# Eight-sublayer decoder trunk: the order in which the third and fourth tile of rows take the last four pieces of weights

## Chip, cores and metric

One core of one Trainium2 chip. The time is device microseconds of one execution of the whole program, all weights read from HBM; lower is better.

## What is computed

A trunk of two layers over 512 rows of 1024 float32 values. Each layer is a half-step SwiGLU feed-forward network (FFN, inner width 2816), a token mixer (linear recurrence and differential attention in the first layer, forgetting attention and a convolution in the second), a cross-attention into 256 memory rows, and a second half-step FFN. So eight sublayers end in all, and each is wrapped the same way:

```
h = h + w * RMSNorm_post(f(RMSNorm_pre(h)))
```

Every matrix product is made to nearly float32 precision out of three passes: both operands are split into a rounded part and a rest (`whi`, `wlo` for weights, `xhi`, `xlo` for inputs), and hi·lo, lo·hi and hi·hi are summed.

## The kernel before

**Data.** `h` stays in SBUF as four tiles of 128 rows (`h[:, t, :]`, t = 0 to 3). A piece of weights is two blocks of 128 x 512. SP loads pieces into 4 raw slots (`load`, L522), ScalarE writes `whi` and VectorE `wlo` into 4 split slots (`split`, `split_next`, L783, L1310 where a norm's gain is multiplied in, L779, L1305 where not), three pieces ahead of use. TensorE counts `pieces_used`; ScalarE's split of piece n waits in L776 until piece n - 4 has been used, and VectorE's half follows ScalarE's. SP reloads a raw slot once the low parts of its piece are made.

**A sublayer's last stage.** The product that ends a sublayer (`mix_out`, `xo`, `down`) has two groups, one for each half of the 1024 output columns. A group has four pieces (`down` five), and tile t sums into bank t of the group's four banks. Its second group is written by `last_group` (L2229), which orders TensorE's work by hand for the last four pieces: tile 0 takes all four, then tile 1 takes all four, then come tiles 2 and 3. When a tile is complete `tile_done` is signalled; for tile 3 the last `pieces_used` serves.

**What runs beside it.** `close_sublayer` exists on ScalarE (L840) and VectorE (L1439); both lists are executed strictly in the order written. For each tile: VectorE adds the product to `y_rows` (only for `down`, L1446), ScalarE squares it with a sum (L829), VectorE makes the variance (L1450) and multiplies the post gain in (L1457), GpSimd raises to -1/2 (L680), VectorE updates `h[t]` (L1492). Then TensorE transposes the tile of h (L2140, eight transposes), ScalarE copies the result to `xhi` (`open_hi`, L814) and VectorE makes `xlo` (`open_lo`, L1338): the next sublayer's input. ScalarE also squares the new h (`next_h`, L818) for the next norm. Between these steps stand the splits of the next stage's first pieces. The last group before nothing (`opens` false) has only the updates and stores.

There are two forms of this. Where the next stage is a gate and up stage (`rows` true; three of the seven), the transposes take rows already scaled by their own norm: VectorE adds to the squares (L1526), GpSimd takes the power (L685), ScalarE writes `y_rows` (`scale_rows`, L867), and only then can TensorE transpose (`scaled_units`, L2148). ScalarE's order there is

```
square_tile 0, next_h(0), scale_rows(0), square_tile 1,
split_next,  next_h(1), open_hi(0), scale_rows(1),
split_next,  open_hi(1), square_tile 2,
split_next,  square_tile 3, next_h(2), scale_rows(2), next_h(3), ...
```

Elsewhere (`rows` false, four of the seven) TensorE transposes h itself (`updated_units`, L2143) and ScalarE's order is

```
square_tile 0, next_h(0), square_tile 1, open_hi(0),
split_next,  next_h(1), open_hi(1),
split_next,  square_tile 2, split_next, square_tile 3, ...
```

VectorE's list has the same shape, with `split_next` at the same places; `update(2)` stands behind `add_second(3)`, the addition of tile 3, in both and in the last one. The `split_next` behind square_tile 1 is the one that needs the slot of the first of the last four pieces; the next ones need the second and third.

**The next stage** begins with `first_group` (L2263): each piece takes tiles 0 and 1 first (256 columns, once `xlo` of both is there) and later tiles 2 and 3. The transposes of tiles 2 and 3 stand between its pieces, behind its second and third piece with `rows`, behind its first and second without.

Of the kernel before, what the change touches and what calls it, by code (L numbers as in the profile page):

```python
# [127 lines left out]
def build(nc, A, out):  # L128
# [9 lines left out]
    def place(name, shape, dt=f32, at=None, size=FLOAT):  # L138

        n = (int(np.prod(shape[1:])) * size + 31) // 32 * 32  # L140
        if at is None:
            at = top[0]
            top[0] += n
        assert at + n <= nc.sbuf_usable_end, (name, at + n - nc.sbuf_usable_end)
        return nc.alloc_sbuf_tensor_at(name, shape, dt, offset=at)
# [48 lines left out]
    rows = place("rows", [P, 3, P], f32, at(9984))  # L194
# [64 lines left out]
    def sem(name):  # L259
# [8 lines left out]
    hi_made, lo_made, pieces_used = map(sem, ("hi_made", "lo_made", "pieces_used"))  # L268
# [22 lines left out]
    tile_done, y_ready, y_squared, proj_ready, v_ready, y_mixed = map(sem, (  # L291
        "tile_done", "y_ready", "y_squared", "proj_ready", "v_ready", "y_mixed"))
# [41 lines left out]
    def group_pieces(kind, g, n, arg=None):  # L334

        return 1 if kind == "odd_in" and ODD_COLS[g][0] == "c_f" else \
            n + 2 if arg == "late_kv" and g == 0 else n
# [156 lines left out]
    def x_bank(t, group):  # L494

        return 4 * ((group + t // 2) % 2)
# [1555 lines left out]
    def _(pe):  # L2052
        E = Engine(pe, None)
# [78 lines left out]
        def wait_banks(group):  # L2132
            wait_evicted(group)
            wait_read(group)

        def x_units(t, bank, bs=(0, 1), src=h):

            for b in bs:
                for k in range(4):
                    last = T(x_unit(bank, t, b)[:, k, :], src[:, t, (4 * b + k) * P:(4 * b + k + 1) * P], ident[:])  # L2140
                E.run(last, x_transposed)

        def updated_units(t):  # L2143

            E.await_(h_ready)
            x_units(t, x_bank(t, E.group))

        def scaled_units(t):  # L2148

            E.await_(h_ready)  # L2150
            E.await_(rows_scaled)
            x_units(t, x_bank(t, E.group), src=y_rows)
# [76 lines left out]
        def last_group(bank, n_kp, src_hi, src_lo, ready, opens, rows):  # L2229

            base, lead = E.piece, n_kp - SPLIT_SLOTS

            def piece(kp, tiles):
                weights(base + kp)
                ready(kp)
                return token_major((base + kp) % SPLIT_SLOTS, kp, n_kp, bank, src_hi, src_lo, tiles)
            for kp in range(lead):
                piece(kp, range(TT)).then_inc(pieces_used, 1)
            for t in range(2):
                for kp in range(lead, n_kp):  # L2240
                    last = piece(kp, (t,))
                E.run(last, tile_done)
            E.group += 1
            if opens and not rows:
                wait_banks(E.group)
                updated_units(0)
            for kp in range(lead, lead + 2):
                piece(kp, (2, 3)).then_inc(pieces_used, 1)
                if rows and kp == lead:
                    wait_banks(E.group)  # L2250
                    scaled_units(0)
            if opens and not rows:
                updated_units(1)
            for kp in range(lead + 2, n_kp):
                last = piece(kp, (2,))
                if rows and kp == lead + 2:
                    scaled_units(1)
            E.run(last, tile_done)
            for kp in range(lead + 2, n_kp):
                piece(kp, (3,)).then_inc(pieces_used, 1)  # L2260
            E.piece += n_kp

        def first_group(ended, rows=False):  # L2263
# [89 lines left out]
        def weights(n):  # L2353

            pe.wait_ge(lo_made, n + 1 + RAW_SLOTS)
# [11 lines left out]
        def token_major(slot, kp, n_kp, bank, src_hi, src_lo, tiles):  # L2367

            for i in range(PK):
                k = 2 * kp + i  # L2370
                for t in tiles:
                    toks = slice(t * P, (t + 1) * P)
                    last = three(PS[:, bank + t, :], src_hi[:, k, toks], src_lo[:, k, toks],
                                 whi[:, slot, i, :], wlo[:, slot, i, :], kp + i == 0,
                                 kp == n_kp - 1 and i == PK - 1)
            return last

        def forget_gates(slot, bank):

            w = [t[:, slot].rearrange("p a (b n) -> p (a b) n", n=P) for t in (whi, wlo)]  # L2380
            for k in range(KT):
                last = three(PS[:, bank, :], w[0][:, k, :], w[1][:, k, :], xhi[:, k, :], xlo[:, k, :],
                             k == 0, k == KT - 1)
            return last
# [29 lines left out]
        for n_stage, (kind, l, arg, ng, np_) in enumerate(STAGES):  # L2414
# [41 lines left out]
            for g in range(straight(kind, ng)):  # L2456
# [6 lines left out]
                n_kp = group_pieces(kind, g, np_, arg)  # L2463
# [3 lines left out]
                if ends_sublayer(kind, arg) and g == 1:  # L2467
                    if arg == "late_kv":
                        E.await_(kv_copied)
                    if kind == "down":  # L2470
                        last_group(bank, n_kp, plain_hi, plain_lo,
                                   lambda kp: pe.wait_ge(mid_lo_ready, 2 * (m0 + kp + 1)), opens(n_stage), opens_scaled(n_stage))
                    else:
                        last_group(bank, n_kp, xhi, xlo, lambda kp: pe.wait_ge(xlo_ready, x_ready + 2 * kp + 2),
                                   opens(n_stage), opens_scaled(n_stage))
                    ended = True
                    continue
# [3 lines left out]
                for n_piece in range(n_kp):  # L2481
                    kp = (0, 1, 0, 1, 2, 3)[n_piece] if late else n_piece
# [8 lines left out]
                    if kind == "down":  # L2491
                        pe.wait_ge(mid_lo_ready, 2 * (m0 + kp + 1))
                        last = token_major(slot, kp, n_kp, bank, plain_hi, plain_lo, range(TT))
                    else:
                        pe.wait_ge(xlo_ready, x_ready + (KT if name == "c_f" else 2 * kp + 2))
                        last = forget_gates(slot, bank) if name == "c_f" else \
# [49 lines left out]
            if kind == "even_in":  # L2546
# [17 lines left out]
                for n in range(len(LEVELS) + 1):  # L2564
# [7 lines left out]
                    for half in range(2):  # L2572
                        if n >= 1:
                            pe.wait_ge(level_merged, 2 * n - 1 + half)
                        for b in range(8 * half, 8 * half + 8):
# [3 lines left out]
                            last = mm(blocks_of(level_bank, level_bank + 4)[:, b, :], lhs, rhs, start=True, stop=True)  # L2579
# [172 lines left out]
```

## Time and profile before

| | us |
|---|---|
| median of 3 runs | 2327.05 |
| lowest, highest | 2322.51, 2327.62 |
| the profiled execution | 2327.22 |
| its span, first to last instruction | 2325.4 |
| TensorE busy | 2301.9 |
| VectorE busy | 1313.6 |
| ScalarE busy | 976.0 |
| GpSimd busy | 77.3 |
| mean granted TensorE clock | 0.997 |

PE is TensorE, PEld its weight load, DVE VectorE, ACT ScalarE, POOL GpSimd. A row of a timeline gives the start in the span, the duration, the engine, the line of the kernel and the operation, and in brackets how long the engine sat idle before it and what ended that. Matmuls are pipelined: the next begins before the one before it ends.

### The profile page before, as it was taken

The numbers are of one execution on the slowest core, as the hardware profiler recorded it, in microseconds if no ns is written. First come the engines' busy times: TensorE is split into PE (matmuls) and PEld (weight loads), VectorE is DVE, ScalarE is ACT, GpSimd is POOL, SyncE is SP. The second block draws the span as 40 slices with busy tenths as digits, with TensorE's granted clock in tenths as the row PEclk, the third lists the DMA queues.
The fourth block names the chain that finished last, engine by engine and source line by source line (L and its number), as shares of the span: only waits on it lengthen the run. The fifth ranks groups of instructions, "written<-read, shape, count | busy, mean of one in ns | idle before, by whom it ended". The sixth has DMA issues, their size and how long they took to land. (4 is left out here: it accounts for less than half of the span.)

```text
span 2325.4 us, 30178 instructions
## 1 busy us (share of the span) xinstructions
PE 2301.9 (99%) x11939; PEld 1951.6 (84%) x11939; DVE 1313.6 (56%) x1833; ACT 976.0 (42%) x1618; POOL 77.3 (3%) x115
## 2 busy tenths in 40 slices
PE   8999999999999999999999999999999999999998
PEld 7888888888888888888888888888888888888887
DVE  5756545595645446573355573355895545567434
ACT  4433324444544454443343443344365445344332
POOL 0000004000000000000010000000000000000000
PEclk9999999999999999999999999999999999999999
DMA  4332232311223122423223313233322222331321
GB/s 167 104 132 81 92 109 79 104 63 55 83 76 106 58 83 96 146 72 94 98 91 109 132 50 118 91 96 96 100 74 73 91 64 91 109 127 55 114 95 72
DMA packets 171650, 217.70 MB, mean 94 GB/s; under 512 B 13080, under 2 KB 123000, under 8 KB 171512
## 3 DMA queue, kind: packets, MB, share of 16 engines
q1 hardware_dynamic: 171400, 215.75, 28.8%
q8 instruction: 96, 1.57, 0.3%
q14 instruction: 42, 0.34, 0.0%
q10 hardware_dynamic: 112, 0.03, 0.0%
HBM read 213.63 MB, written 2.10 MB: 93 GB/s over the span
## 5 line engine op out<-in xcount | busy, mean ns | idle before, releaser
L2058 PE MATMUL ps<-xlo,whi 128*128 128x512 f32 (+1 forms) x2056 | 756.7, 368 | 1.7 <-DVE wlo L1310 1.7
L2059 PE MATMUL ps<-xhi,wlo 128*128 128x512 f32 (+1 forms) x2056 | 753.6, 367 | 0.0
L2060 PE MATMUL ps<-xhi,whi 128*128 128x512 f32 (+1 forms) x2056 | 753.5, 366 | 0.0
L1310 DVE SCALAR_TENSOR_TENSOR wlo<-raw,vec,whi 128x512 fp32r<-128x512 f32 (+1 forms) x488 | 340.8, 742 | 397.0 <-ACT whi L783 395.9
L783 ACT ACTIVATE whi<-raw,vec 128x512 fp32r<-128x512 f32 (+1 forms) x488 | 320.8, 709 | 456.7 <-PE ps L2060 394.4
L2058 PEld LDWEIGHTS ps<-xlo,whi 128*128 128x128 f32 x2056 | 389.1, 189 | 64.7 <-issue 2.1
L2059 PEld LDWEIGHTS ps<-xhi,wlo 128*128 128x128 f32 x2056 | 389.1, 189 | 62.4
L2060 PEld LDWEIGHTS ps<-xhi,whi 128*128 128x128 f32 x2056 | 388.9, 189 | 62.6
L1305 DVE TENSOR_TENSOR wlo<-raw,whi 128x1024 fp32r<-128x1024 f32 x104 | 126.8, 1223 | 188.5 <-ACT whi L779 187.7
L779 ACT ACTIVATE whi<-raw 128x1024 fp32r<-128x1024 f32 x104 | 109.5, 1056 | 209.8 <-PE ps L2060 209.3
L2058 PE MATMUL ps<-wlo,xhi 128*128 128x512 f32 x352 | 139.7, 397 | 2.5 <-issue 2.5
L2059 PE MATMUL ps<-whi,xlo 128*128 128x512 f32 x352 | 137.9, 392 | 0.0
L2060 PE MATMUL ps<-whi,xhi 128*128 128x512 f32 x352 | 137.8, 392 | 0.0
L2176 PE MATMUL ps<-wlo,mid_hi 128*128 128x512 f32 x336 | 131.6, 392 | 0.4 <-DVE wlo L1299 0.4
L2180 PE MATMUL ps<-whi,mid_lo 128*128 128x512 f32 x336 | 130.8, 389 | 0.0
L2181 PE MATMUL ps<-whi,mid_hi 128*128 128x512 f32 x336 | 130.8, 389 | 0.0
L2058 PE MATMUL ps<-wlo,plain_hi 128*128 128x512 f32 x320 | 125.0, 391 | 0.0
L2060 PE MATMUL ps<-whi,plain_hi 128*128 128x512 f32 x320 | 124.6, 389 | 0.0
L2059 PE MATMUL ps<-whi,plain_lo 128*128 128x512 f32 x320 | 124.5, 389 | 0.0
L802 ACT ACTIVATE whi<-w 128x512 fp32r<-128x512 f32 x144 | 83.3, 622 | 91.9 <-PE ps L2060 33.9
L1299 DVE TENSOR_TENSOR wlo<-w,whi 128x512 fp32r<-128x512 f32 x144 | 92.9, 685 | 35.3 <-ACT whi L802 34.4
L1736 DVE TENSOR_TENSOR mid<-mid,ps 128x1024 f32<-128x1024 f32 x33 | 40.3, 1221 | 111.9 <-ACT mid L1058 111.9
(279 smaller groups left out, 2842.3 us busy)
## 6 DMA issues: line engine op xcount, KB each, us to landing
raw<-ffn_w_gate_dram SPq DMA_DIRECT2D x176, 256.0 KB, 2.8
raw<-ffn_w_up_dram SPq DMA_DIRECT2D x176, 256.0 KB, 3.1
raw<-ffn_w_down_dram SPq DMA_DIRECT2D x96, 256.0 KB, 3.0
w<-ffn_w_down_dram SPq DMA_DIRECT2D x72, 256.0 KB, 5.2
raw<-xattn_w_kv_dram SPq DMA_DIRECT2D x64, 256.0 KB, 2.9
raw<-even_w_in_dram SPq DMA_DIRECT2D x56, 256.0 KB, 2.9
raw<-odd_w_in_dram SPq DMA_DIRECT2D x42, 256.0 KB, 2.9
raw<-xattn_w_q_dram SPq DMA_DIRECT2D x32, 256.0 KB, 3.0
```

Of the source, the lines that this page charges most:

```text
L779: a(flat(whi[:, slot]), flat(raw[:, from_slot]), ACT.Copy).then_inc(hi_made, 1)
L783: last = a(hi[:, k, :], full[:, k, :], ACT.Copy, scale=vec[:, c:c + 1])
L802: last = a(whi[:, slot, i, :], unit_source(k, name, q), ACT.Copy)
L1299: last = v.tensor_tensor(wlo[:, slot, i, :], unit_source(k, name, q), whi[:, slot, i, :].bitcast(f32), SUB)
L1305: v.tensor_tensor(flat(wlo[:, slot]), flat(raw[:, from_slot]), flat(whi[:, slot]).bitcast(f32), SUB).then_inc(lo_made, 1)
L1310: last = v.scalar_tensor_tensor(out=lo[:, k, :], in0=full[:, k, :], scalar=vec[:, c:c + 1], in1=hi[:, k, :].bitcast(f32), op0=MUL, op1=SUB)
L2058: mm(out_ap, lh, rl, start=start, stop=False, skip_group_check=skip_group_check)
L2059: mm(out_ap, ll, rh, start=False, stop=False, skip_group_check=skip_group_check)
L2060: return mm(out_ap, lh, rh, start=False, stop=stop, skip_group_check=skip_group_check)
L2176: opening = mm(out, hi, wlo[:, slot, i, :], start=fresh, stop=False, skip_group_check=True)
L2180: mm(out, lo, whi[:, slot, i, :], start=False, stop=False, skip_group_check=True)
L2181: last = mm(out, hi, whi[:, slot, i, :], start=False, stop=ends, skip_group_check=True)
```

## The change

Only the order of TensorE's work in `last_group` behind tile 1 changes. Before, tiles 2 and 3 take the first two of the last four pieces together (piece by piece), then tile 2 takes the other two, then tile 3. After, tile 2 takes all four pieces, then tile 3 takes all four, and each piece is counted as used behind its step of tile 3. The transposes of the next input keep their places counted in steps: tile 0's scaled transposes come behind two steps, tile 1's behind five; without scaled rows before the first and behind the fourth.

```diff
--- before.py
+++ after.py
@@ -2244,20 +2244,18 @@
             if opens and not rows:
                 wait_banks(E.group)
                 updated_units(0)
-            for kp in range(lead, lead + 2):
-                piece(kp, (2, 3)).then_inc(pieces_used, 1)
-                if rows and kp == lead:
+            for kp in range(lead, n_kp):
+                last = piece(kp, (2,))
+                if rows and kp == lead + 1:
                     wait_banks(E.group)
                     scaled_units(0)
+            E.run(last, tile_done)
             if opens and not rows:
                 updated_units(1)
-            for kp in range(lead + 2, n_kp):
-                last = piece(kp, (2,))
-                if rows and kp == lead + 2:
+            for kp in range(lead, n_kp):
+                piece(kp, (3,)).then_inc(pieces_used, 1)
+                if rows and kp == lead:
                     scaled_units(1)
-            E.run(last, tile_done)
-            for kp in range(lead + 2, n_kp):
-                piece(kp, (3,)).then_inc(pieces_used, 1)
             E.piece += n_kp
 
         def first_group(ended, rows=False):
```

## Rows read from the trace of the kernel before

**Rows 1.** PE's line in the page: busy time, share of the span, instructions
```profile
PE 2301.9 (99%) x11939; PEld 1951.6 (84%) x11939; DVE 1313.6 (56%) x1833; ACT 976.0 (42%) x1618; POOL 77.3 (3%) x115
```

**Rows 2.** Timeline of PE, first cross-attention's end: start, us, instruction, [idle before <-releaser]
```profile
838.65 0.39 PE L2060 MATMUL ps<-whi,xhi 128*128 128x512 f32 x1
...
843.62 0.39 PE L2060 MATMUL ps<-whi,xhi 128*128 128x512 f32 x1
843.94 1.06 PE L2140 MATMUL ps<-ident,y_rows 128*128 128x128 f32 x8
...
846.00 0.39 PE L2060 MATMUL ps<-whi,xhi 128*128 128x512 f32 x1
...
848.95 0.28 PE L2058 MATMUL ps<-xlo,whi 128*128 128x256 f32 x1
...
854.71 1.04 PE L2140 MATMUL ps<-ident,y_rows 128*128 128x128 f32 x8
```

**Rows 3.** Timeline of ACT, the same end
```profile
839.14 1.34 ACT L783 ACTIVATE whi<-raw,vec 128x512 fp32r<-128x512 f32 x2 [1.57 <-PE ps L2060]
840.38 1.05 ACT L818 ACTIVATE h_scratch<-h 128x1024 f32<-128x1024 f32 x1
...
841.42 1.06 ACT L814 ACTIVATE xhi<-ps 128x512 fp32r<-128x512 f32 x2
842.64 1.16 ACT L867 ACTIVATE y_rows<-h,rstd_in 128x1024 f32<-128x1024 f32 x1 [0.16 <-POOL rstd_in L685]
843.70 1.32 ACT L783 ACTIVATE whi<-raw,vec 128x512 fp32r<-128x512 f32 x2
...
852.74 1.16 ACT L867 ACTIVATE y_rows<-h,rstd_in 128x1024 f32<-128x1024 f32 x1 [1.83 <-POOL rstd_in L685]
```

**Rows 4.** Timeline of DVE, the same end
```profile
845.05 1.41 DVE L1310 SCALAR_TENSOR_TENSOR wlo<-raw,vec,whi 128x512 fp32r<-128x512 f32 x2 [1.73 <-ACT whi L783]
846.38 1.28 DVE L1338 TENSOR_TENSOR xlo<-ps,xhi 128x512 fp32r<-128x512 f32 x2
```

**Rows 5.** Timeline of PE, end of the first layer's second FFN
```profile
1200.69 1.06 PE L2140 MATMUL ps<-ident,y_rows 128*128 128x128 f32 x8 [0.65 <-ACT y_rows L867]
...
1212.97 1.06 PE L2140 MATMUL ps<-ident,y_rows 128*128 128x128 f32 x8 [1.36 <-ACT y_rows L867]
```

**Rows 6.** Timeline of ACT, the same end
```profile
1200.45 1.32 ACT L783 ACTIVATE whi<-raw,vec 128x512 fp32r<-128x512 f32 x2
```

**Rows 7.** Timeline of PE, end of the first FFN
```profile
371.10 0.39 PE L2060 MATMUL ps<-whi,plain_hi 128*128 128x512 f32 x1
...
378.30 1.04 PE L2140 MATMUL ps<-ident,h 128*128 128x128 f32 x8
```

**Rows 8.** Timeline of DVE, the same end
```profile
372.05 1.42 DVE L1310 SCALAR_TENSOR_TENSOR wlo<-raw,vec,whi 128x512 fp32r<-128x512 f32 x2 [0.42 <-ACT whi L783]
...
376.53 1.28 DVE L1492 SCALAR_TENSOR_TENSOR h<-y_rows,rstd,h 128x1024 f32<-128x1024 f32 x1 [0.21 <-DVE y_rows L1446]
```

**Rows 9.** Timeline of DVE, end of the first layer's mixer
```profile
721.42 0.16 DVE L1450 SCALAR_TENSOR_TENSOR var<-result_squares 128x1 f32<-128x1 f32 x1
...
722.30 1.28 DVE L1492 SCALAR_TENSOR_TENSOR h<-y_rows,rstd,h 128x1024 f32<-128x1024 f32 x1
```

**Rows 10.** Timeline of PE, the same end
```profile
726.09 1.04 PE L2140 MATMUL ps<-ident,h 128*128 128x128 f32 x8
```

**Rows 11.** Timeline of DVE, end of the last FFN
```profile
2319.07 1.28 DVE L1492 SCALAR_TENSOR_TENSOR h<-y_rows,rstd,h 128x1024 f32<-128x1024 f32 x1 [0.21 <-DVE y_rows L1446]
```

**Rows 12.** Timeline of PE, kernel start and last matmul
```profile
12.81 0.55 PE L2058 MATMUL ps<-xlo,whi 128*128 128x256 f32 x1 [1.74 <-DVE wlo L1310]
...
18.50 0.41 PE L2060 MATMUL ps<-xhi,whi 128*128 128x256 f32 x1
...
2317.74 0.39 PE L2060 MATMUL ps<-whi,plain_hi 128*128 128x512 f32 x1
```

**Rows 13.** One slice: busy us by engine, then granted PE clock, DMA
```profile
2322.00:2323.00 1.00, 0.00 (x0) 0.00 (x0) 0.95 (x2) 0.00 (x0) 0.00 (x0) 0.94 0.49 197
```

## Prediction

> **What bounds the kernel now.** The page comes first: TensorE is busy 99% of the span [rows 1], so any time in which it waits for something is lost one for one, and nothing that only fills ScalarE or VectorE counts. The change keeps all 96 matmuls of the last four pieces, so only waits can come or go. I then laid the timelines of TensorE, ScalarE, VectorE and GpSimd over each of the eight ends of a sublayer. At seven of them the next sublayer's input is made while the last group still runs, and two strict orders meet: ScalarE's and VectorE's list in `close_sublayer`, and the slots of split weights. The step of ScalarE's list behind its square of tile 1, the split of the next stage's first piece, waits for the slot of the first of the four last pieces (L776), and everything of tile 1 stands behind it. So the view that decides is not the waits in total (TensorE's waits for scaled rows are 0.65 and 1.36 us, [rows 5]) but ScalarE's timeline just after that release.
>
> **What the change moves.** Count a step as one tile times one piece, six matmuls; from [rows 2] (846.00 to 848.95: twelve matmuls and one more start) a matmul takes 0.227 us, a step 1.36. Before, the four slots come free after steps 10, 12, 15 and 16 and tile 2 is done after step 14. After: slots at 13, 14, 15 and 16, tile 2 at 12. The transposes keep their places (tile 0's after step 10 or before step 9, tile 1's after step 13 or 12). No instruction is added or removed, no DMA either. The first slot therefore comes 4.97 us later (838.65 to 843.62, transposes included [rows 2]), the second 2.7 plus whatever has been added by then.
>
> **A, ends that open gate and up with scaled rows (three: both cross-attentions, first layer's second FFN).** Times are those of [rows 2 to 4]. Step 13's last matmul ends at 843.62 + 0.39 = 844.01; ScalarE starts the split 0.10 later, as it does now (838.65 + 0.39 to 839.14 [rows 3]). From that start the chain is fixed: split 1.24, square of h 1.04, tile 0's high parts, then the scaled rows of tile 1, which begin 3.50 after the split and take 1.16. So they are ready at 844.11 + 3.50 + 1.16 = 848.77, and with the usual 0.15 the transposes of tile 1 start at 848.92, not 843.94: **+4.98**. TensorE itself is what is queued behind that wait: steps 14 to 16.
> Step 14 then frees the second slot at 848.92 + 2.06 + 0.39 = 851.37 (distance 843.94 to 846.00 [rows 2]), and ScalarE splits at 851.47 instead of 843.70, 7.77 later. VectorE's low parts follow 1.35 behind, tile 1's low input 1.33 behind that and takes 1.28 [rows 4]: ready at 855.43. The next sublayer's first matmul needs it; it would want to start at 848.95 + 4.98 = 853.93, so it waits again: **+6.5** by then. Tile 2's whole chain on VectorE hangs on the same step, so its scaled rows (852.74 + 1.16 [rows 3]) come 7.77 later, at 861.67, and its transposes at 861.82 against 854.71 [rows 2]: **+7.1 for the end**. Tile 3 and the rest had over a microsecond of slack or move with TensorE: nothing more. The other cross-attention end has the same distances.
> The FFN end [rows 5, 6]: TensorE already waits 0.65 for tile 1 and 1.36 for tile 2, so no slack. Step 13 ends at 1200.69 - 0.65 = 1200.04; split at 1200.14; transposes 3.50 + 1.16 + 0.15 later, 1204.95, **+4.26**. Second slot at 1204.95 + 2.45, split at 1207.50 against 1200.45 [rows 6]: +7.05, passed in full to tile 2's transposes. **+7.0 for the end.** Sum of the three: 21.2.
>
> **B, ends of an FFN that open a mixer (two)** [rows 7, 8]. Here tile 1's transposes don't wait for ScalarE, so TensorE isn't stopped inside the group. Step 13 ends at 371.10 + 0.39; split 371.59, square of h +1.24, tile 1's high parts +1.04, second split about 0.98 later (two copies of 1.06 in all, less the overlap [rows 3]) at 374.85, VectorE's low parts 1.35 after it at 376.20, against 372.05 now: +4.15. Tile 2's addition stands behind that on VectorE (the earlier tile_done, 2.7 us, is useless: it waits in line). h of tile 2 is now ready at 376.53 + 1.28 = 377.81, after at 381.96; TensorE wants it at 378.30. With some 0.07 for the wait, **+3.7 each, 7.4.**
>
> **C, ends of a mixer that open cross-attention (two)** [rows 9, 10]. Same PE order, so the first split starts at 719.38 (step 13's last matmul lies 7.20 ahead of tile 2's transposes as in B: 726.09 - 7.20 = 718.89, and 0.49 to the split) and the second low split at 719.38 + 1.24 + 1.04 + 0.98 + 1.35 = 723.99. The next instruction follows 1.33 later, then variance to update 0.88 (721.42 to 722.30), update 1.28: 727.48, transposes about 727.55 against 726.09. **+1.5 each, 3.0.** There is no addition on VectorE, hence the smaller price.
>
> **D, the last end** [rows 11]. Tile 2 is done 2.7 us sooner, but the update of its h is written behind the addition of tile 3, for which it waits today (0.21 behind it). Nothing: 0, at best -1 if that wait were not the one.
>
> Later reloads of raw slots go out up to 7.8 us later, but TensorE is as late, and ScalarE waits for TensorE there, not for data: 0.
>
> **The clock, which the trace bounds only.** The stall inside A's group leaves TensorE idle from 844.01 to 848.92, 4.9 us, three times. In the trace the granted clock stays 1.00 after the last matmul (end 2318.13 [rows 12]) and is 0.94 in the slice from 2322, so it is on its way from the 2.4 GHz level to 0.5, the 1.2 GHz level, about 4.8 us after it [rows 13]; behind the idle 1.36 the matmuls are as short as ever. What slow time costs is read from the start of the kernel: 256-column matmuls take 0.41 instead of 0.28 [rows 2, 12], one per 0.213 us instead of 0.12, from 12.81 to 18.7, so 5.9 us of work at about half speed, 2.95 lost. Bounds: 0 and 3 x 2.95 = 8.9. Between them I take one fall of three at about 2.2, nearer to none than to three, since in that row the full clock lasted nearly as long as the stall does.
> By a rule of the Trainium skill (TensorE: Matmul & The Clock Gate, section "HAM oscillation — how this bites in real kernels") waits of a few microseconds between bursts of matmuls throttle the array again each time; by it all three stalls count, which is rival 1.
>
> **Sum.** 21.2 + 7.4 + 3.0 + 0 + 2.2 = 34. The profiled execution took 2327.22 (span 2325.4), the median 2327.05, so nothing is to be corrected: 2361. Without any fall it is 2359.
>
> **Rivals.**
> 1. The clock falls at all three stalls: 31.6 + 8.9, 2368. For it: the stall is as long as the idle time before the fall in [rows 13]. Against it: in that row the clock was still full for nearly all of it, so a stall of 4.9 is at the edge. 0.15.
> 2. The stalls don't add up: only the wait inside A's group counts, and later waits fall within slack that I have read too small (0.66 us before tile 2's transposes in A, 0.5 in B). 3 x 4.7 = 14, 2341. Against it: the FFN end's idle 1.36 [rows 5] shows none. 0.08.
> 3. The later slots are covered: the first comes free 4.1 us (three steps) before the group's end and both halves of a split take 2.7, so weights are never late. 2327. For it: its one wait for split weights is the 1.74 us at the start [rows 12]. Against it: the splits aren't what is late, but what stands behind them. That the change does not do what it says belongs here; I see no way for it. 0.04.
> 4. Faster: tile 2 is finished 2.7 us sooner and its chain is what ends last at the FFN's end (1.36) and in the tail (up to 1): -2.4, 2324.7. It decides from the moment that ScalarE and VectorE take tile 2 before they meet the late slot; in the program they take it behind two splits. 0.03.
> The forecast itself: 0.70.
>
> A measurement of this kernel tells about 0.2%, 4.6 us, from no change; case 2 and 1 are far above. Slower: 0.70 + 0.15 + 0.08 = 0.93, within 0.04, faster 0.03. The range: the forecast's own spread is from 2353 (each chain a microsecond shorter at seven ends, no fall) to 2367; with case 1 it reaches 2370. Low end 2351, which leaves out cases 2 to 4, 0.15.
>
> **What would show it.** In the profile of the changed kernel: at A, tile 1's transposes idle 4.9 (FFN 4.9 as well) and tile 2's again (about 0.5 and 2.6), the first matmul of the next sublayer idle 1.6 behind xlo; at B idle 3.3 at tile 2's transposes and 0.4 before them, at C 0.4 and 1.1; ScalarE's first gained split starting right at step 13; h updates of tile 2 never earlier than now; no idle at the tail. TensorE's total waits should be some 32 us more, with the clock 1.00 except behind those stalls. It is wrong if tile 1's transposes don't wait at A, or if TensorE's matmuls themselves take longer.

## The result and the profile after

The changed kernel takes 2364.86 us (2360.77 to 2367.80, five runs) against 2327.05 (2322.51 to 2327.62, five runs): a ratio of 1.0165, 95% interval 1.0153 to 1.0177, 37.8 us slower. The forecast was 2361 with a range of 2351 to 2370. The profiled execution is the quickest of the five, 2360.77 us with a span of 2359.0, so the traces account for 33.6 us of the 37.8; what the other runs have on top comes up again below.

The page's line on TensorE answers to [rows 1]:

```profile
PE 2308.5 (98%) x11939; PEld 1954.2 (83%) x11939; DVE 1313.2 (56%) x1833; ACT 974.7 (41%) x1618; POOL 77.3 (3%) x115
```

TensorE's own busy time is 6.6 us more, the span 33.6: most of it is waiting, 26.9 us by the sums of the waits in the two traces. The waits of TensorE in the changed kernel (engine, line, what for: us in total, times, longest):

```profile
PE ps L2140 <- ACT y_rows L867: 17.7, 6, 4.9
PE ps L2140 <- DVE h L1492: 7.4, 4, 2.9
...
PE ps L2058 <- issue: 6.3, 11, 1.0
```

The first row was 2.0 in two waits before [rows 5], the second did not exist. "issue", where the profile names nothing that was waited for, grew from 2.5 us in four waits to 6.3 in eleven. The seven new ones stand before the first matmul of the next sublayer, which needs `xlo`: 0.86 to 0.97 at the three scaled ends, 0.28 at the four others.

**Ends with scaled rows.** TensorE at the first cross-attention's end, answering to [rows 2]:

```profile
846.12 0.39 PE L2060 MATMUL ps<-whi,xhi 128*128 128x512 f32 x1
851.40 1.94 PE L2140 MATMUL ps<-ident,y_rows 128*128 128x128 f32 x8 [4.89 <-ACT y_rows L867]
852.99 0.78 PE L2058 MATMUL ps<-wlo,xhi 128*128 128x512 f32 x1
...
860.08 0.35 PE L2058 MATMUL ps<-xlo,whi 128*128 128x256 f32 x1 [0.87 <-issue]
...
866.36 0.85 PE L2140 MATMUL ps<-ident,y_rows 128*128 128x128 f32 x6 [0.30 <-ACT y_rows L867]
```

and ScalarE beside it, answering to [rows 3]:

```profile
846.60 1.33 ACT L783 ACTIVATE whi<-raw,vec 128x512 fp32r<-128x512 f32 x2 [6.54 <-PE ps L2060]
...
850.10 1.15 ACT L867 ACTIVATE y_rows<-h,rstd_in 128x1024 f32<-128x1024 f32 x1 [0.17 <-POOL rstd_in L685]
855.99 1.34 ACT L783 ACTIVATE whi<-raw,vec 128x512 fp32r<-128x512 f32 x2 [4.74 <-PE ps L2060]
...
865.06 1.15 ACT L867 ACTIVATE y_rows<-h,rstd_in 128x1024 f32<-128x1024 f32 x1 [1.83 <-POOL rstd_in L685]
```

Read them together. The last matmul of step 13 starts at 846.12 and ends 0.39 later; the split starts 0.09 behind that; 3.50 later come tile 1's scaled rows, and the transposes start 4.89 us after TensorE ran dry. The chain is the one written down. What isn't is the column of durations: transposes and matmuls behind the stall last 1.94 and 0.78 instead of 1.06 and 0.48. The slices of this stretch (columns as in [rows 13], the third number from the right is the granted clock) show why:

```profile
849.00:850.00 1.00, 0.00 (x0) 0.00 (x0) 0.96 (x3) 0.94 (x2) 0.47 (x1) 1.00 0.00 0
850.00:851.00 1.00, 0.00 (x0) 0.00 (x0) 0.78 (x2) 0.90 (x1) 0.07 (x1) 0.55 0.40 77
851.00:852.00 1.00, 0.60 (x3) 0.64 (x4) 0.00 (x0) 0.25 (x1) 0.00 (x0) 0.50 1.02 354
...
856.00:857.00 1.00, 1.00 (x4) 0.72 (x4) 0.00 (x0) 1.00 (x2) 0.00 (x0) 0.54 0.00 0
857.00:858.00 1.00, 1.00 (x6) 0.82 (x5) 0.64 (x1) 1.00 (x3) 0.00 (x0) 1.00 0.00 0
```

TensorE is idle from 846.5; the clock goes to the 1.2 GHz level during 850 and stays there to the beginning of 857, through all the slices between. The second slot comes free with it: ScalarE's second split is 9.39 after its first (855.99 to 846.60), where the forecast without the clock had 7.36 (844.11 to 851.47). From the second split the rest follows as written. `xlo` of tile 1 is ready at 858.69 + 1.28 = 859.97, and the next sublayer starts at 860.08; tile 2's rows are ready at 866.21, its transposes start at 866.36. VectorE there:

```profile
858.69 1.28 DVE L1338 TENSOR_TENSOR xlo<-ps,xhi 128x512 fp32r<-128x512 f32 x2
```

At the FFN's end (to [rows 5]):

```profile
1216.62 1.94 PE L2140 MATMUL ps<-ident,y_rows 128*128 128x128 f32 x8 [4.89 <-ACT y_rows L867]
...
1225.30 0.36 PE L2058 MATMUL ps<-xlo,whi 128*128 128x256 f32 x1 [0.86 <-issue]
...
1233.76 1.07 PE L2140 MATMUL ps<-ident,y_rows 128*128 128x128 f32 x8 [2.47 <-ACT y_rows L867]
```

**Ends without scaled rows.** The first FFN's end and the second layer's (to [rows 7]), and the first mixer's (to [rows 10]), all of TensorE:

```profile
374.48 0.35 PE L2058 MATMUL ps<-xlo,whi 128*128 128x256 f32 x1 [0.28 <-issue]
...
380.52 1.10 PE L2140 MATMUL ps<-ident,h 128*128 128x128 f32 x8 [2.94 <-DVE h L1492]
```

```profile
1590.46 1.69 PE L2140 MATMUL ps<-ident,h 128*128 128x128 f32 x8 [2.93 <-DVE h L1492]
```

```profile
724.63 0.36 PE L2058 MATMUL ps<-xlo,whi 128*128 128x256 f32 x1 [0.28 <-issue]
...
728.49 1.09 PE L2140 MATMUL ps<-ident,h 128*128 128x128 f32 x8 [0.75 <-DVE h L1492]
```

VectorE shows why the mixer's end waits less. At the first FFN's end two additions stand between the second low part and tile 2's update:

```profile
376.13 0.68 DVE L1446 TENSOR_TENSOR y_rows<-ps,y_rows 128x512 f32<-128x512 f32 x1
...
378.28 0.68 DVE L1446 TENSOR_TENSOR y_rows<-ps,y_rows 128x512 f32<-128x512 f32 x1
379.18 1.28 DVE L1492 SCALAR_TENSOR_TENSOR h<-y_rows,rstd,h 128x1024 f32<-128x1024 f32 x1 [0.21 <-DVE y_rows L1446]
```

and at the first mixer's end there is none:

```profile
727.15 1.28 DVE L1492 SCALAR_TENSOR_TENSOR h<-y_rows,rstd,h 128x1024 f32<-128x1024 f32 x1
```

From the start of the second low part (374.79 and 724.94) to the end of this update it is 5.67 us at the FFN's end and 3.49 at the mixer's. The 2.18 between them is the difference of the two waits, 2.94 and 0.75.

**The last end.** VectorE, to [rows 11]:

```profile
2351.75 0.69 DVE L1446 TENSOR_TENSOR y_rows<-ps,y_rows 128x512 f32<-128x512 f32 x1 [3.19 <-PE ps L2060]
2352.66 1.28 DVE L1492 SCALAR_TENSOR_TENSOR h<-y_rows,rstd,h 128x1024 f32<-128x1024 f32 x1 [0.21 <-DVE y_rows L1446]
```

Nothing has changed there: tile 2's update still stands behind tile 3's addition.

The price of each end can be read off without the rest of the run: take the distance from tile 0's transposes to tile 3's in both traces. The second profile of the changed kernel is that of the run changed_again.

| end | opens | before | after | added | second profile, added | forecast without the clock |
|---|---|---|---|---|---|---|
| first FFN | mixer | 19.31 | 22.97 | 3.66 | 5.21 | 3.7 |
| first mixer | cross-attention | 19.29 | 20.80 | 1.51 | 1.51 | 1.5 |
| first cross-attention | gate and up | 19.57 | 28.76 | 9.19 | 9.19 | 7.1 |
| first layer's second FFN | gate and up | 21.83 | 30.94 | 9.11 | 10.60 | 7.0 |
| second layer's first FFN | mixer | 19.31 | 24.53 | 5.22 | 5.17 | 3.7 |
| second mixer | cross-attention | 19.30 | 20.80 | 1.50 | 1.51 | 1.5 |
| second cross-attention | gate and up | 19.58 | 28.75 | 9.17 | 8.70 | 7.1 |
| sum | | | | 39.4 | 41.9 | 31.6 |

The sum is 39.4 us and the span grew by 33.6. The rest was given back in places that the change doesn't touch: 1.4 at the start, 1.3 inside the first layer's mixer and 3.1 inside the second's. At the start the matmuls are slow for a different time: in the kernel before, those of 256 columns come 0.213 us apart from 12.81 to 18.7 [rows 12], in the changed kernel's profile only for 3.4 us. The kernel before has a stretch of low clock in each mixer, in the second it looks like this (slices, same columns):

```profile
1787.00:1788.00 1.00, 1.00 (x7) 1.00 (x6) 0.00 (x0) 0.00 (x0) 0.00 (x0) 0.50 0.00 0
1790.00:1791.00 1.00, 1.00 (x4) 0.81 (x3) 0.71 (x1) 0.00 (x0) 1.00 (x1) 0.50 0.00 0
...
1794.00:1795.00 1.00, 1.00 (x6) 0.83 (x5) 0.00 (x0) 0.00 (x0) 0.00 (x0) 1.00 0.00 0
```

6.8 us at half clock in each. The changed kernel's profile has 3.4 us of it in the first mixer and none in the second:

```profile
1809.00:1828.00 19.00, 19.00 (x128) 17.44 (x127) 7.91 (x11) 8.81 (x12) 1.93 (x1) 1.00 0.27 94
```

In changed_again both mixers have 6.8 us at half clock and give nothing back, and its span is 40.7 us longer than before. So this part differs from execution to execution. last_end below shows it without the change, since its work is that of the kernel before up to the last end: it is 1.5 us earlier at the first FFN's end, and its first mixer, with 10.2 us at half clock, takes 1.4 us longer. The profiled run has a mean granted clock of 0.993, the other four 0.990 to 0.992, and it lies 4 us under the median.

### The profile page after: what moved, and what is told of

The parts are those of the page before. It is cut to its first block and busy times, and to the rows that moved or that the text cites. A ratio compares the mean times of both kernels' runs of the same rounds, so it can differ in the third digit from the quotient of the medians.

```text
span 2359.0 us, 30194 instructions
## 1 busy us (share of the span) xinstructions
PE 2308.5 (98%) x11939; PEld 1954.2 (83%) x11939; DVE 1313.2 (56%) x1833; ACT 974.7 (41%) x1618; POOL 77.3 (3%) x115
```

## Experiments

Theory Q: a slot of split weights that comes free later holds up, in ScalarE's and VectorE's ordered lists, everything that stands behind the split, and long waits of TensorE bring the clock down on top. Against it: late weights as such, the new order of tiles as such, and a clock that only matters by chance. Each median is compared with the kernel before on the same chip: 2326.18 for scaled_ends, plain_ends, late_slots and split_behind, 2326.25 for filled_stall, last_end, lists_old_order and lists_for_new_order, 2326.47 for changed_again and lists_new_order_2.

**Parts of the change alone.** `last_group` has both orders and takes the new one only where a condition holds:

```diff
+            if rows:
+                (new order)
+            else:
+                (old order)
```

> The new order only at the three ends with scaled rows, the old one at the others. Theory Q (the price is what stands behind the late slot in ScalarE's and VectorE's lists, 7.1, 7.0 and 7.1 us, and the clock's fall in each 4.9 us stall, 2.1 each): +27, so 2351 to 2357, with tile 1's scaled transposes idle 4.9 at all three ends. Rival W (late weights and reloads, spread over all seven ends alike): three sevenths of 37.8, +16, 2343. Rival C (the clock only matters by chance, the order costs 21): 2348.

Measured 2352.73 (2352.34 to 2353.30), ratio 1.0114 (1.0097 to 1.0131): +26.6. Rival W (2343) is out, and rival C (2348), by which the clock matters only by chance, is nearly 5 us off.

With `opens and not rows` as the condition:

> The new order only at the four ends without scaled rows that something follows. Theory Q: 2 x 3.7 + 2 x 1.5 = +10.4, up to 1.6 more for each FFN end at which the clock falls: 2336 to 2341, tile 2's transposes idle 2.9 at the FFN ends and 0.75 at the mixers' ends, nothing at the scaled ends beyond what they have. Rival W (spread alike): four sevenths of 37.8, +22, 2349.

Measured 2338.47 (2334.83 to 2339.15), ratio 1.0050 (1.0035 to 1.0065): +12.3, between the 10.4 without any fall and the 13.6 with two. The profiled execution is the quickest of the four, 2334.83, and the clock held at both of its FFN ends: they cost 3.7 each. The waits of its profile are those of theory Q, the scaled rows' wait is that of before:

```profile
PE ps L2140 <- DVE h L1492: 7.4, 4, 2.9
...
PE ps L2140 <- ACT y_rows L867: 2.0, 2, 1.3
```

With `not opens`:

> The new order only in the last end, behind which nothing follows. Theory Q: 0, because the update of tile 2 is written behind the addition of tile 3: 2326 to 2328. Rival E (tile 2's 2.7 us are worth something in the tail): 1 to 2 us faster.

Measured 2327.13, ratio 1.0003 (0.9994 to 1.0011). Tile 2 is indeed done earlier, and it brings nothing; VectorE's timeline shows where it waits:

```profile
2314.24 0.68 DVE L1457 TENSOR_TENSOR y_rows<-y_rows,post_gain 128x512 f32<-128x512 f32 x1
2318.13 0.69 DVE L1446 TENSOR_TENSOR y_rows<-ps,y_rows 128x512 f32<-128x512 f32 x1 [3.20 <-PE ps L2060]
2319.03 1.28 DVE L1492 SCALAR_TENSOR_TENSOR h<-y_rows,rstd,h 128x1024 f32<-128x1024 f32 x1 [0.21 <-DVE y_rows L1446]
```

The gain multiply of tile 2 is over at 2314.9 and its update starts at 2319.03, behind the addition of tile 3. The three parts add to 26.6 + 12.3 + 0.9 = 39.8; the whole change is 37.8 and, measured again, 39.0. So nothing is lost or won between the ends.

**Only the slots late.** The tiles in the old order, the counts moved:

```diff
-                piece(kp, (2, 3)).then_inc(pieces_used, 1)
+                piece(kp, (2, 3))
...
+            piece(lead + 2, (2,)).then_inc(pieces_used, 1)
...
+            E.run(piece(lead + 3, (2,)), tile_done)
+            piece(lead + 2, (3,)).then_inc(pieces_used, 2)
+            piece(lead + 3, (3,)).then_inc(pieces_used, 1)
```

> The old order of tiles (the first two pieces shared by tiles 2 and 3, tile 2 done behind step 14), but the slots counted free behind steps 13, 15, 15 and 16. Theory Q: the late slot is the whole cause and the early tile 2 worth nothing, so as slow as the changed kernel or a little slower, since the second slot is a step later: 2362 to 2374, tile 1's scaled transposes idle 4.9. Rival O (the order of the matmuls itself, or tile 2's early end colliding with other steps, carries a part): clearly faster than the changed kernel, under 2355.

Measured 2370.84 (2370.57 to 2372.17), ratio 1.0193 (1.0178 to 1.0208). The order of the tiles is not what costs: with the old order and late counts the kernel is 44.7 us slower, 6 us beyond the changed one, and its second slot comes one more step late. ScalarE at the first cross-attention's end:

```profile
850.10 1.33 ACT L783 ACTIVATE whi<-raw,vec 128x512 fp32r<-128x512 f32 x2 [6.54 <-PE ps L2060]
...
861.06 1.34 ACT L783 ACTIVATE whi<-raw,vec 128x512 fp32r<-128x512 f32 x2 [6.32 <-PE ps L2060]
```

From the first split to the second it is now 10.96 us instead of 9.39.

**The same late slots with nothing behind them.** The changed kernel; at the scaled ends ScalarE and VectorE take the first split behind tile 1's work:

```diff
                 square_tile(kind, second, 1, done + n)
-                split_next()
                 next_h(1)
                 open_hi(0, x_bank(0, E.group))
                 scale_rows(1)
                 split_next()
+                split_next()
...
                 update(1, take(1))
-                split_next()
                 row_variance(1)
                 open_lo(0, x_banks[0])
                 split_next()
+                split_next()
```

> The new order, and at the three scaled ends both lists take the first split behind tile 1's work (ScalarE behind scale_rows(1), VectorE behind row_variance(1) and open_lo(0)); the slot stays as late. Theory Q: the 4.9 us stall goes and with it the clock's falls; what stays at these ends is tile 1's low input behind two splits, about 2 to 3 us each: 17 to 22 us slower than before, 2344 to 2349. Rival W (late weights are what costs): no change against the changed kernel, 2365.

Measured 2345.73 (2343.55 to 2348.32), ratio 1.0084 (1.0069 to 1.0100): of 37.8 us 18 are gone, with slots that come free after the same step. ScalarE at the first cross-attention's end:

```profile
847.23 1.15 ACT L867 ACTIVATE y_rows<-h,rstd_in 128x1024 f32<-128x1024 f32 x1
849.51 1.34 ACT L783 ACTIVATE whi<-raw,vec 128x512 fp32r<-128x512 f32 x2 [1.13 <-PE ps L2060]
851.77 1.34 ACT L783 ACTIVATE whi<-raw,vec 128x512 fp32r<-128x512 f32 x2 [0.92 <-PE ps L2060]
853.01 1.06 ACT L814 ACTIVATE xhi<-ps 128x512 fp32r<-128x512 f32 x2
```

The scaled rows are ready before the first slot is free, TensorE goes on without the stall, and the three ends cost 2.1, 2.8 and 2.1 (from the distances as in the table) instead of 9.2, 9.1 and 9.2. What is left is the second half: tile 1's high part (853.01) still stands behind both splits.

The same lists in the kernel before:

> The kernel before with the lists of split_behind. Theory Q: here the slot is free long before, so the lists bring little: the waits of 0.65 and 1.36 us at the first layer's second FFN may go or grow by a microsecond, 2325 to 2329. Rival L (the lists were bad in any case, and split_behind gains by them and not by the late slot): 10 us or more faster than before.

Measured 2328.16 (2325.49 to 2329.11), ratio 1.0005 (0.9996 to 1.0014): no difference. The gain of split_behind is that of an undone stall and not of better lists. One wait even grew, that of tile 2's transposes at the FFN's end, from 1.36 to 2.47; that the second split now stands close behind the first is the likely reason, and no run tests it alone.

**The clock by itself.** The changed kernel with work that fills the stall at the scaled ends:

```diff
                 if rows and kp == lead:
+                    held = whi[:, (base + lead + 1) % SPLIT_SLOTS, 0, :]
+                    for _ in range(16):
+                        mm(PS[:, x_bank(1, E.group) + 2, :], ident_r[:], held, start=True, stop=True)
                     scaled_units(1)
```

> The changed kernel with 16 more matmuls of 512 columns in front of tile 1's scaled transposes at the three scaled ends (into the banks that these transposes then overwrite): 3.6 of the 4.9 us of waiting are filled. Theory Q with the clock: the waits stay, the clock doesn't fall there, 3 x 2.1 = 6.3 less than the changed kernel, 2357 to 2360, and the six matmuls behind the transposes take 0.39 instead of 0.78. Rival C (the falls cost nothing, since the chain through ScalarE is the bound in any case): as the changed kernel, 2364 to 2366.

Measured 2357.73 (2356.73 to 2359.25), ratio 1.0135 (1.0121 to 1.0149). Sixteen matmuls more at each of the three ends, and still 7.1 us faster than the changed kernel's 2364.86. TensorE, and the slice in which step 14 runs:

```profile
849.86 3.79 PE L2260 MATMUL ps<-whi,ident_r 128*128 128x512 f32 x16
854.91 1.06 PE L2140 MATMUL ps<-ident,y_rows 128*128 128x128 f32 x8 [1.27 <-ACT y_rows L867]
855.74 0.48 PE L2058 MATMUL ps<-wlo,xhi 128*128 128x512 f32 x1
```

```profile
855.00:856.00 1.00, 1.00 (x9) 1.00 (x10) 0.00 (x0) 0.00 (x0) 0.00 (x0) 1.00 0.89 309
```

Compare 0.48 and 1.00 with 0.78 and 0.50 above. TensorE still waits 1.27 for the same rows. By their own comparisons with the kernel before it is +31.5 here and +37.8 and +39.0 for the changed kernel. The three ends cost 7.15, 7.07 and 7.14 here; the forecast without the clock said 7.1, 7.0 and 7.1.

**The changed kernel again:**

> The changed kernel itself, as a bound for filled_stall, scaled_ends and plain_ends on one chip: 2361 to 2368. Theory Q with the clock: low granted clock behind each of the three 4.9 us stalls in this profile too, at the FFN ends (2.9 us idle) in some profiles only.

Measured 2365.51 (2363.74 to 2368.19), ratio 1.0167 (1.0151 to 1.0182). Its profile (2366.1 span) has the low clock at all three scaled ends, at both FFN ends that open a mixer, and a second time at the FFN end that opens gate and up, behind the wait for tile 2: the column of the table above.

**Is there something in the new order?** All lists rewritten for it: tile 2's chain ahead of the splits.

```diff
+                square_tile(kind, second, 2, done + n)
                 split_next()
                 open_hi(1, x_bank(1, E.group))
+                split_next()
+                next_h(2)
...
+                update(2, take(2))
                 split_next()
                 open_lo(1, x_banks[1])
```

> The new order with all lists rewritten for it: tile 2's square, variance, gain and update stand ahead of the splits, the splits behind tile 1's copy, GpSimd's power of the scaled tile 2 ahead of tile 3's, and in the last end tile 2's update ahead of tile 3's addition. Theory Q: the late slots then hide (two splits of 2.7 us in 4.1 us ahead of the group's end), the waits of 0.65 and 1.36 go and 0.6 in the tail: 2323 to 2327. Rival W: the weights are late all the same, over 2335.

Measured 2328.67 (2325.95 to 2330.37), ratio 1.0008 (0.9999 to 1.0017): the 38 us are gone, but the expected 2323 to 2327 is missed. Its profile shows new waits of my own making: for tile 3's scaled rows (0.7, 0.9 and 0.7 us), for `xlo` at the FFN's end (1.0), and 0.4 for `wlo` at each FFN end that opens a mixer. The longest for `wlo`, 2.2, is the one at the kernel's start (1.7 before):

```profile
PE ps L2055 <- DVE wlo L1310: 2.9, 3, 2.2
PE ps L2137 <- ACT y_rows L867: 2.9, 4, 0.9
...
PE ps L2055 <- DVE xlo L1338: 1.0, 1, 1.0
```

With tile 3's square and update ahead of the third split, and tile 1's low input ahead of tile 2's update elsewhere:

> As lists_for_new_order, with its own new waits mended: at the scaled ends tile 3's square and update stand ahead of the third split (tile 3's transposes were idle 0.7 to 0.9), at the others tile 1's low input ahead of tile 2's update (the next sublayer's first matmul came later by 0.6). Theory Q: TensorE is left with 16 us of waits less 2 and the tail 0.6 shorter, 2323 to 2326. Rival F (the order of tiles is worth nothing to a kernel that is never late): within 0.1% of before.

Measured 2326.19 (2323.35 to 2328.13), ratio 0.9995 (0.9986 to 1.0004). The expected 2323 to 2326 is missed by 0.2, and what rival F says, within 0.1% of before, is what was measured. The waits at the ends are down:

```profile
PE ps L2055 <- DVE xlo L1338: 1.0, 1, 1.0
...
PE ps L2137 <- ACT y_rows L867: 0.6, 1, 0.6
```

and the tail between tile 3's addition and the last update is 2.80 us instead of 3.36, but at the FFN's end the idle 1.36 for tile 2 has only made room for the idle 1.0 in front of the first matmul. All of it, 0.9 us by the distances and the tail, is less than a measurement can tell. No version found beats the kernel before.

## Why the prediction came out as it did

**The chain at the scaled ends: right.** The first slot 4.97 later, tile 1's transposes 4.98 later (measured 4.96: the lag behind the old trace goes from 2.50 to 7.46; at the FFN's end 4.26 forecast, 4.24 measured), a second wait before the next sublayer (1.6 forecast, 1.47 with the clock held in filled_stall) and a third for tile 2, 7.1, 7.0 and 7.1 in all: filled_stall gives these numbers with the clock held, 7.15, 7.07 and 7.14. split_behind shows that it is what stands behind the split, late_slots that it is the slot and not the order.

**The FFN ends and the mixers' ends: right.** 3.7 forecast and 3.66 measured where the clock held, 1.5 forecast and 1.50 and 1.51 measured. The reason given for the difference between them, VectorE's addition, is the one that its rows show: 5.67 us of work behind the second split there, 3.49 here.

**The last end: right**, 0 (last_end).

**The clock: mis-sized.** The term that was wrong is "I take one fall of three at about 2.2". It fell at all three scaled ends, in both profiles of the changed kernel and in those of scaled_ends and late_slots. In the changed kernel's profiles one fall inside the group cost 1.6 to 2.0 (9.19 or 8.70 against the 7.15 and 7.14 of filled_stall), in place of an upper bound of 2.95, and 1.3 at the first cross-attention's end of scaled_ends. A fall costs less than half of the time at half clock, because only the slow work up to the second slot's release counts (9.39 us from split to split in place of 7.36); what is slow behind it falls into the later waits. The reason given for one in three doesn't hold either. It was one row, [rows 13], in which the clock stayed full for 4.8 us behind the last matmul. In the slices above it is low from about 850.1, 3.6 us after TensorE ran dry. Over the twelve stalls of these four profiles it fell 2.1 to 5.0 us after, and behind the last matmul of the kernel, in the profiles of all the kernels here, 2.1 to 5.3 us after: one row was one draw.

And I had left the clock out where the waits are shorter: at the two FFN ends that open a mixer (wait 2.9) it was low in three of the four cases of the table, 5.2 instead of 3.7, and in changed_again a second time behind the wait for tile 2 at the other FFN end, 10.60. In the profile the term is 39.4 - 31.6 = 7.8, in the second 10.3, against 2.2 in the sum. The forecast was near all the same, and that is partly luck: in the profiled execution 5.8 us were given back at the start and in the mixers, of which the sum knew nothing; in changed_again, where 1.2 came back, the execution took 2368.19. The median, 2364.86, lies 3.8 over the forecast. Rival 1 (a fall at every one of the three, 2368) was right about how often and wrong about the price. The rule of the Trainium skill that stood beside it (TensorE: Matmul & The Clock Gate, "HAM oscillation — how this bites in real kernels") agrees with these traces for the waits of 4.9 us: each of the twelve brought the granted clock down, to 0.50 in the slices above. The waits of 2.9 us did so in some cases only, as said.

**The signs named beforehand.** Total waits were to grow by some 32 us with the matmuls as fast as before; they grew by 26.9, and the other 6.6 of the 33.6 are slower matmuls. The prediction calls itself wrong if the matmuls themselves take longer. Where the clock held each end cost what was written down, so this is the clock's term again: slow matmuls were allowed for behind the three stalls, and not behind the waits of 2.9 us.

**Rivals 2, 3 and 4: out.** The later waits do add up (2), the 4.1 us between the slot and the group's end do cover the splits, as lists_new_order_2 shows, but not the list behind them (3), and an earlier tile 2 is worth nothing as long as its chain is written behind the splits, and less than can be measured when it is written ahead of them (4).

## What to carry to other kernels

When the release of a shared buffer is moved, look for the instruction that waits for it on every engine and price everything written behind that instruction, not the buffer's own consumer: here the weights were never late, and tile 1's scaled rows were. Walking the lists with durations of the old trace gave each end to 0.1 us wherever the clock held. A wait of several microseconds on TensorE should be priced with the slow matmuls behind it as well, and a profile of one execution may have stretches of low clock in other places than the next one, so compare distances inside a stage before comparing spans.

## What the hardware showed that was not expected

The clock is not only brought down by the long stalls. Behind a wait of 2.93 us at the second layer's first FFN it went to 0.5 when the transposes were already running (slices of the changed kernel, columns as before):

```profile
1588.00:1589.00 1.00, 0.00 (x0) 0.00 (x0) 0.90 (x2) 0.75 (x3) 0.70 (x1) 1.00 0.91 336
1590.00:1591.00 1.00, 0.54 (x4) 0.54 (x5) 1.00 (x4) 0.56 (x1) 0.45 (x1) 0.90 0.00 0
1591.00:1592.00 1.00, 1.00 (x7) 1.00 (x6) 1.00 (x3) 1.00 (x3) 0.48 (x1) 0.50 0.00 0
```

while the same wait of 2.94 at the first FFN's end left it at 1.00 in this profile and brought it down in changed_again. Six profiles have this wait at both of these ends (also late_slots, filled_stall, split_behind and plain_ends); the clock fell in eight of the twelve cases. The kernel before, with no wait over 0.7 us there, has 6.8 us at half clock in each mixer, where TensorE runs many small matmuls; the profiles of the experiments, which leave the mixers alone, have 10.2, 6.8, 3.4 or none there. In the kernel before both stretches begin during or 0.4 us behind 32 matmuls of one column each (L2110, 581.46 to 585.14 and 1784.67 to 1789.38; the clock falls at about 585.5 and 1787.0). The changed kernel's profile has the same 32 in its second mixer, from 1810.76, and no fall, and no run tests whether they are the reason. And at the start of the kernel before, the matmuls are slow ([rows 12]) while the granted clock of that stretch reads 1.00; in the changed kernel's profile it reads 0.5 there. Why the record differs stays open. So does what decides in which execution a wait of 2.9 us brings the clock down.
